# A two-layer pair of transformer blocks in one kernel: ScalarE's forget-gate steps one place later, and the layer change in another order

## The reference, cut to what matters

```python
# end of the first and of the second layer
x = _layernorm(ALPHA * x + y, ln_w[layer], ln_b[layer])

# third layer, the gated linear one
proj = h @ w_in                                  # 2048 -> 8192: q, fz, i, gate
log_f = jnp.logaddexp(jnp.log(lb), jnp.log1p(-lb) + jax.nn.log_sigmoid(fz))
k = (1.0 - lb) * jax.nn.sigmoid(-fz)
b = jnp.cumsum(gc, axis=-2)                      # gc: log_f, per head and key column
A = jnp.einsum('bhtd,bhsd,bhtsd->bhts', qc, kc, decay)
```

## Time and profile before

| | |
|---|---|
| runs | 1857.69, 1857.76, 1859.28 us; median 1857.76 us |
| the profiled execution: own time | 1856.62 us |
| its span | 1854.8 us, so 1.8 us lie around it |
| PE busy | 1828.5 us, 99% of the span |
| PEld busy | 1533.8 us (83%) |
| DVE busy | 1259.7 us (68%) |
| ACT busy | 956.4 us (52%) |
| weight transfers | 315.88 MB read from HBM, 171 GB/s |

### The profile page before, as it was taken

The page is one execution under the profiler, slowest core; times in us unless marked ns, Lnnn a source line. Parts: engine busy times, 40 slices in busy tenths (PEclk is TensorE's granted clock), DMA queues, the critical chain, the costliest instruction groups (busy, mean ns, idle before and its releaser), DMA issues.

```text
span 1854.8 us, 24335 instructions
## 1 busy us (share of the span) xinstructions
PE 1828.5 (99%) x8827; PEld 1533.8 (83%) x8827; DVE 1259.7 (68%) x1692; ACT 956.4 (52%) x1323; POOL 38.2 (2%) x114
## 2 busy tenths in 40 slices
PE   8999999999999999999999999999999999999999
PEld 6888888887888888887787887878888888888887
DVE  5566666588557755768787868777766555577764
ACT  4555554455455545536554545545435444565542
POOL 2000000000000004000000000000000000000000
PEclk9999999999999999999999999999999999999999
DMA  8555454667789887665554554544556666545453
GB/s 276 170 170 149 137 170 143 212 179 167 183 153 211 176 182 165 202 236 155 167 171 145 161 170 147 171 146 159 175 148 204 183 191 191 160 150 173 155 170 114
DMA packets 169867, 319.25 MB, mean 172 GB/s; under 512 B 16264, under 2 KB 20512, under 8 KB 169008
## 3 DMA queue, kind: packets, MB, share of 16 engines
q1 hardware_dynamic: 168656, 313.69, 58.7%
q10 hardware_dynamic: 576, 4.19, 0.5%
q0 software_dynamic: 544, 0.13, 0.1%
HBM read 315.88 MB, written 2.10 MB: 171 GB/s over the span
## 4 chain that ended last, share of the span: by engine, by line
PE 48%; DVE 2%; issue 1%; ACT 0%; DVEq 0%; ACTq 0%
PE acc L298 14%; PE acc L300 14%; PE acc L299 14%; PE ps L2656 2%; PE ps L540 1%; DVE arena L2043 1%; PE ps L393 0%; PE ps L2645 0%; PE ps L2742 0%; DVE wlo L267 0%; PE ps L2637 0%; PE ps L573 0%; ACT whi L259 0%; DVE arena L2030 0%; DVE arena L2031 0%
## 5 line engine op out<-in xcount | busy, mean ns | idle before, releaser
L267 DVE TENSOR_TENSOR wlo<-wraw,whi 128x1024 fp32r<-128x1024 f32 (+1 forms) x595 | 714.9, 1216 | 377.5 <-ACT whi L259 374.5
L259 ACT ACTIVATE whi<-wraw 128x1024 fp32r<-128x1024 f32 (+1 forms) x595 | 613.1, 1046 | 333.1 <-PE acc L300 330.6
L298 PE MATMUL acc<-whi,ta_hi 128*128 128x512 f32 x1664 | 662.4, 398 | 12.3 <-DVE wlo L267 12.3
L300 PE MATMUL acc<-whi,ta_lo 128*128 128x512 f32 x1664 | 650.3, 391 | 0.0
L299 PE MATMUL acc<-wlo,ta_hi 128*128 128x512 f32 x1664 | 649.8, 390 | 0.0
L298 PEld LDWEIGHTS acc<-whi,ta_hi 128*128 128x128 f32 x1664 | 313.8, 189 | 78.7 <-DVE wlo L267 14.0
L300 PEld LDWEIGHTS acc<-whi,ta_lo 128*128 128x128 f32 x1664 | 313.5, 188 | 66.9
L299 PEld LDWEIGHTS acc<-wlo,ta_hi 128*128 128x128 f32 x1664 | 314.1, 189 | 62.1
L298 PE MATMUL acc<-whi,tb_hi 128*128 128x512 f32 (+1 forms) x704 | 276.7, 393 | 0.0
L300 PE MATMUL acc<-whi,tb_lo 128*128 128x512 f32 (+1 forms) x704 | 271.5, 386 | 0.0
L299 PE MATMUL acc<-wlo,tb_hi 128*128 128x512 f32 (+1 forms) x704 | 271.1, 385 | 0.0
(11 more groups left out here) (314 smaller groups left out, 1354.3 us busy)
## 6 DMA issues: line engine op xcount, KB each, us to landing
wraw<-in_ml_w_in SPq DMA_DIRECT2D x129, 512.0 KB, 5.8
wraw<-in_a_w_in SPq DMA_DIRECT2D x128, 512.0 KB, 3.9
wraw<-in_kv_w SPq DMA_DIRECT2D x64, 512.0 KB, 3.8
wraw<-in_b_w_in SPq DMA_DIRECT2D x64, 512.0 KB, 4.3
wraw<-in_mla_w_in SPq DMA_DIRECT2D x49, 512.0 KB, 4.5
wraw<-in_mla_w_out SPq DMA_DIRECT2D x32, 512.0 KB, 3.8
wraw<-in_ml_w_out SPq DMA_DIRECT2D x32, 512.0 KB, 4.5
wraw<-in_a_w_out SPq DMA_DIRECT2D x32, 512.0 KB, 3.7
```

Source lines behind the costliest of these rows:

```text
L259: nc.scalar.activation(unit_of(whi, n, SPLIT, w), unit_of(wraw, n, RAW, w), ACT.Copy).then_inc(w_high, 1)
L267: nc.vector.tensor_tensor(unit_of(wlo, n, SPLIT, w), unit_of(wraw, n, RAW, w), unit_of(whi, n, SPLIT, w).bitcast(F32), ALU.subtract).then_ ...
L298: nc.tensor.matmul(o, xh, wh, start=first, stop=False)
L300: m = nc.tensor.matmul(o, xl, wh, start=False, stop=end)
```

## The change

Three engines' lists are reordered; no instruction is added or taken out. In stage `l2` ScalarE's exp and ln of the forget gates move from behind the query copy at u = 19 to behind `high` of the unit at u = 20. In the layer change all three lists are rearranged, on VectorE the residual of block 1 is taken out of `ln_stats` and stands by itself further ahead.

```diff
@@ ScalarE, ln_change
                 ln_rstd(n, 0)
-                split(0)
-                split(1)
+                for p in range(3):
+                    split(p)
                 affine(0, 0)
                 hi(0, 0)
                 hi(0, 1)
                 affine(0, 2)
+                split(3)
                 hi(0, 2)
                 ln_rstd(n, 1)
-                split(2)
                 affine(0, 3)
                 hi(0, 3)
                 affine(1, 0)
                 hi(1, 0)
-                split(3)
                 affine(1, 2)
                 hi(1, 1)
+                split(4)
                 hi(1, 2)
-                split(4)
                 affine(1, 3)
                 hi(1, 3)
@@ ScalarE, l2_side
                     nc.scalar.activation(flat(qT2), ps2(0), ACT.Copy).then_inc(l2["qT"], 1)
+
+                def forget():
                     act.wait_ge(l2["nf"], 1 + g)
                     nc.scalar.activation(dT[:, 0, :], dT[:, 0, :], ACT.Exp).then_inc(l2["lf"], 1)
...
                 if u == L2_AT["turn"] + LAG:
                     turned()
+                if u == L2_AT["turn"] + LAG + 1:
+                    forget()
@@ VectorE, ln_stats and ln_change
-                last_residual(name, b)
                 last_stats(name, b)
...
+                last_residual(done, 0)
                 ln_stats(n, done, 0)
                 ln_scale(n, 0, 0, 1)
                 ln_scale(n, 0, 1, 4)
                 split(0)
                 affine(0, 1)
+                last_residual(done, 1)
                 lo(0, 0)
+                split(1)
                 ln_stats(n, done, 1)
                 lo(0, 1)
+                split(2)
+                ln_scale(n, 1, 0, 1)
                 lo(0, 2)
-                ln_scale(n, 1, 0, 1)
-                split(1)
-                split(2)
+                split(3)
                 ln_scale(n, 1, 1, 4)
                 lo(0, 3)
                 lo(1, 0)
                 affine(1, 1)
-                split(3)
                 lo(1, 1)
                 lo(1, 2)
                 split(4)
@@ TensorE, ln_change
-                last(1, 0)
-                last(1, 1)
-                for q in range(3):
-                    ln_turn(n, 0, q)
-                last(1, 2)
+                for i in range(3):
+                    last(1, i)
+                ln_turn(n, 0, 0)
+                ln_turn(n, 0, 1)
                 last(1, 3)
+                ln_turn(n, 0, 2)
+                ln_turn(n, 0, 3)
                 pe.wait_ge(tr_lo, at + 1)
                 new(0, 0)
-                ln_turn(n, 0, 3)
-                ln_turn(n, 1, 0)
                 new(0, 1)
                 pe.wait_ge(tr_lo, at + 2)
                 new(0, 2)
+                ln_turn(n, 1, 0)
+                new(0, 3)
                 for q in range(1, 4):
                     ln_turn(n, 1, q)
                 pe.wait_ge(tr_lo, at + 5)
                 new(1, 0)
                 new(1, 1)
-                new(0, 3)
                 pe.wait_ge(tr_lo, at + 6)
                 new(1, 2)
                 new(1, 3)
```

## The result

| | before | after |
|---|---|---|
| runs, us | 1857.59, 1857.69, 1857.76, 1859.28 | 1841.86, 1841.89, 1841.97, 1843.0 |
| median, us | 1857.72 | 1841.93 |
| the profiled execution: own time, span | 1856.62, 1854.8 | 1841.89, 1840.1 |

The ratio is 0.9915, 95% interval 0.9902 to 0.9927: 15.8 us faster. The forecast was 1842.0 us.

A forecast was written before the change was run, and what follows sets the result against it. PE, busy 99% of the span, bounds the kernel, so only its stops and low clock count. 8.4 + 4.6 + 1.0 + 1.4 = 15.4 us off gives 1842.4, stated as 1842.0 us; 8-in-10 range 1838.8 to 1847.2.

The forecast's parts named there:

- Part 1, order: Forget gates, gated layer: exp and ln behind `high` 20 let PE resume 2.09 us sooner in each group, 8.4 us.
- Part 1, clock: Behind PE's stops in groups 1 to 3: all three low-clock stretches vanish, 3 x 1.53 = 4.6 us.
- the 0.4 us taken off the median: Forecast total: 1842.0 us instead of 1842.4, since part of the runs' spread may be low-clock stretches that vanish too.
- Part 2: The two layer changes: the new order shortens PE's stops, 1.0 us in change 1 and 1.4 in change 0.
- the third, small one: Layer change, before `new(0, 3)`: PE stops a third time, for 0.4 us, about 0.2 in brackets.
- The layer change gives nothing: Rival, both layer changes: stops only change places since VectorE is nearly always busy; 1844.8 us, up to 1846.6; chance 0.14.
- The clock rival: Behind the forget-gate stops: the order works but the clock still falls behind the shorter stop; 1847.0 us; chance 0.08.
- the late semaphore: Forget gates: another semaphore of the string comes up to 1 us later in each group; up to 1846.4 us; chance 0.05.
- late weights: Forget gates: raw weights of `high` 20 land late, delaying exp, ln, scans and `low` 21 in each group; chance 0.01.
- The slower rival: Whole kernel: `high` 20 before exp gets its weights over 6.1 us late; 1861.5 us and more; chance 0.01.

The follow-up runs named there:

- the two stop experiments: The changed kernel with one or two more VectorE subtractions before the scans, lengthening PE's stop in each of four groups: 1846.79 us and 1858.23 us.
- forget_only: The kernel before with only exp and ln of the forget gates moved behind the next weight half, layer changes in the old order: 1844.10 us, ratio 0.9924.
- change1_old_order: The changed kernel with layer change 1 back in the old order on all three engines, change 0 in the new one: 1842.15 us.
- stop_2_9us: The changed kernel with two more VectorE subtractions before the scans, to make PE's stop about 2.9 us in each group: 1858.23 us.

## Why the prediction was right, and where it was not

**Part 1, order.** Forecast 2.09 us a group and 3.62 us in a group with a low stretch; measured 1.98 (group 0), 3.60, 3.58, 3.58. Each step was as worked out: `high` 20 in ScalarE's idle time, exp unmoved, L2042 2.09 us sooner, a remaining stop of 0.27 us for the forecast's 0.28. The forget-gate step alone agrees: 13.8 us, against 8.2 us of order (1.98, and 3.58 to 3.60 less 1.53 in the other groups) and 6.1 us of clock (next point), less about 0.8 for the stretch that two of its four runs have in the layer change: 13.5 us.

**Part 1, clock.** The three stretches went, as forecast, and the two stop experiments show that a stop of 1.5 us leaves the clock alone here and one of 2.8 us does not, in three of four places. Mis-sized was how many stretches there are to win. The profiled execution of before had three. The 19 runs of before beside the first experiments fall into three classes, by mean clock: 0.997 (6 runs, median 1856.07 us), 0.996 (11 runs, 1857.98 us) and 0.995 (2 runs, 1859.7 us). The steps from class to class are 1.9 and 1.7 us, somewhat more than the price of one stretch, 1.53 us. The profile of before with its three stretches is at 0.997, that of the layer changes alone with its four at 0.996. So the usual run has one stretch more than the profiled one, and that is why the profiled one lies 1.1 us below the median (its time, 1856.62 us, is that of its class within the spread of the start-up). For the median the term is then 4 x 1.53 = 6.1 instead of 4.6 us. The prediction had seen this as a possibility (the 0.4 us taken off the median). The rule of the Trainium skill that it cited ("TensorE: Matmul & The Clock Gate", Part 1: the place of the clock's change differs from run to run) agrees with these traces, in which the number of stretches differs as well: the code up to 380 us is the same in before and in the forget-gate step alone, and only the latter's profile has a stretch there; behind like stops in group 0 the clock fell with the layer changes alone and not in before.

**Part 2.** This term was mis-sized, 2.4 us for 1.3. The step that failed is the end of the working for change 1, the sentence "Behind it VectorE's `lo(1, 2)` and `low` 4 end some 0.2 us before PE wants them (859.8): close, but no stop." It is true, and the working stopped there. Up to `new(1, 0)` both changes came out nearly as forecast: from the first residual to `new(1, 0)` it took 16.89 us in each, against 16.34 and 16.84 plus the 1.37 still owed before, so 0.82 us was won in change 1 (forecast 1.0) and 1.32 in change 0 (forecast 1.4). The two stops were 0.86 and 0.77 us in brackets for 0.8 and 0.9; the third, small one did not come. But in change 1 PE then meets the flip matmul, which needs ScalarE's scale, which needs VectorE's work on the stream. PE was ahead by 0.8 us more, VectorE was not. Its lead over before even shrank, from 1.94 us at the residual to 1.20 at its work on the stream (L1693 at 861.29; before, L1691 at 862.49):

```profile
883.20 1.92 ACT L1314 ACTIVATE arena<-x_res 128x2048 f32<-128x2048 f32 x1 [4.65 <-DVE x_res L1688]
...
885.82 0.38 PE L2702 MATMUL ps<-nrm,arena 128*128 128x2 f32 x2 [0.27 <-ACT nrm L1316]
```

```profile
884.57 1.92 ACT L1315 ACTIVATE arena<-x_res 128x2048 f32<-128x2048 f32 x1 [3.44 <-DVE x_res L1686]
```

(First the changed kernel, ScalarE and then PE, two answers of the timeline; then ScalarE before.) The square starts 1.37 us sooner than before, while PE's lead had been 2.76 us at `new(1, 0)`. PE gives back 0.43 us in the stop and 0.29 in slow restarts, half of them behind `new(1, 0)` and half behind the flip matmul. Moving the flip matmul one unit on gives 0.77 us (0.60 in the profiles), and with change 1 back in its old order PE's loss comes back at this very place: both say that this is where the gain of change 1 ended. Change 0 has no such place and kept 1.19 of its 1.32 us.

**The rivals.** "The layer change gives nothing" (0.14) came true for change 1 and not for change 0. The clock rival, the late semaphore and late weights did not occur; the last stays untried, since `high` 20 never waited for data. The slower rival had no sign of it.

**The total.** Runs: 8.2 (order) + 6.1 (four stretches, an estimate from the classes) + 1.3 = 15.6 us, measured 15.8; the rest is less than what the start-up alone varies by. The forecast's 1842.0 had 8.4, 4.6 and 2.4 in place of 8.2, 6.1 and 1.3, and 0.4 off for the spread; the errors cancel.

## What to carry to other kernels

When two engines wait for each other in turn, look for an independent instruction that stands behind the wait and put it before: it fills idle time, and the other engine's chain of steps is free sooner. Where an engine other than the one that bounds the kernel is nearly always busy (VectorE 14.88 of 16 us) a gain has to be followed on to the next place where the bounding engine needs that other one; there it may be taken back. And price a stop with what the clock does behind it, over several runs and not one profile: here more than a third of the runs' gain was clock (6.1 of 15.8 us), and the number of low stretches is most of why the kernel's runs spread over 4 us. When an effect is smaller than the differences of the start-up, compare the start times of the same instruction in two profiles, behind the start-up.

## What the runs showed of the hardware

- Of stops of the same length in one kernel some bring the low clock and some do not. Stops of 2.3 to 2.4 us: groups 1 to 3 but not 0 in the profiled run of before, all four with the layer changes alone. Group 0 of that last run, behind its stop:

```profile
911.00:915.00 4.00, 4.00 (x19) 3.35 (x19) 4.00 (x4) 0.96 (x2) 0.00 (x0) 0.73 0.96 329
```

- Stops up to 1.6 us together with others close by (old layer change) brought it in one of three profiled executions (forget_only; not before, nor change1_old_order with its one old change). Single stops of 1.5 us did not bring it in any of 4 runs, nor did stops of 0.9 and 0.8 us (new layer change) in any of the 9 runs of the changed kernel (mean clock 1.000 in each).
- A low stretch can last longer than one of before: behind the 2.80 us stop of group 1 (stop_2_9us) the mean clock is 0.57 over 8 us, where in the kernel before it was 0.61 over 4 us.
- Matmuls restart slowly behind even a short stop at full clock: 0.18 us are lost besides the 0.43 of the stop itself (group 1 of the changed kernel).
